# HGRN2 levels of the first four heads dealt under the f and q projections of the other four

## What is computed

```python
def hgrn2_mixer(h, w_in, lb, g_norm, w_out):
    proj = h @ w_in
    q_raw, f_raw, i_in, z = split_cols(proj, [HG_K_W, HG_K_W, HG_V_W, HG_V_W])
    q = silu(q_raw); f = lb + (1.0 - lb) * sigmoid(f_raw)
    k = 1.0 - f; logf = log(f); v = i_in          # 8 heads, 128 keys, 128 values
    ...
    # per head: o_t = sum over s <= t of (q_t * prod_{s<r<=t} f_r) . k_s  v_s
    o = o * rsqrt(mean(o * o) + EPS)
    o = o * g_norm
    return (o * silu(z)) @ w_out
```

## Time and profile before

| what | us |
|---|---|
| median of 3 runs (lowest to highest) | 358.63 (356.74 to 360.58) |
| profiled execution, its own time | 356.69 |
| span of the profiled execution | 354.2 |
| TensorE, VectorE, ScalarE, GpSimd busy | 332.1, 233.6, 181.8, 89.7 |
| level stretch | about 269 to 312 |

### The profile page before, as it was taken

One profiled execution on the slowest core, in us unless ns is written; L12 is line 12 of the kernel. 1 busy time (PEld: TensorE's weight loads), 2 busy tenths in 40 slices (PEclk: granted clock), 3 DMA queues, 4 the chain that ended last, 5 costly groups with the idle time before them and its releaser, 6 DMA issues.

```text
span 354.2 us, 5694 instructions
## 1 busy us (share of the span) xinstructions
PE 332.1 (94%) x2157; PEld 281.1 (79%) x2157; DVE 233.6 (66%) x396; ACT 181.8 (51%) x372; POOL 89.7 (25%) x83
## 2 busy tenths in 40 slices
PE   8999779999989969789899999999999999999993
PEld 5789577878979945466568878999999999889882
DVE  3884693566657779675634872744485997799942
ACT  4950556455564597775705654836473010067721
POOL 2012003343201134463420010022061575533000
PEclk9999989999999999999999999999999999999999
DMA  7999699542749000420430277671656015001011
GB/s 288 370 200 295 251 305 212 196 135 104 150 91 217 20 1 2 134 103 3 160 138 0 62 265 262 211 264 35 223 220 240 0 49 190 2 0 43 18 60 59
DMA packets 28474, 49.37 MB, mean 139 GB/s; under 512 B 3160, under 2 KB 7648, under 8 KB 28448
## 3 DMA queue, kind: packets, MB, share of 16 engines
q1 hardware_dynamic: 25696, 44.82, 40.6%
q10 hardware_dynamic: 2240, 2.17, 3.1%
q0 software_dynamic: 512, 2.03, 1.6%
HBM read 47.97 MB, written 1.05 MB: 138 GB/s over the span
## 4 chain that ended last, share of the span: by engine, by line
PE 66%; DVE 13%; ACT 8%; DMA 7%; issue 3%; POOL 1%; SPq 1%; DVEq 0%; ACTq 0%
PE bank L611 62%; DMA raw<-in_nsa 7%; DVE w_lo L1103 5%; PE bank L791 2%; ACT w_hi L882 2%; ACT prob L1002 1%; DVE nmax L1311 1%; POOL prob L532 1%; PE bank L711 1%; ACT h_hi L889 1%; DVE prob_t L1323 1%; ACT w_hi L908 1%; PE bank L852 0%; DVE zT L1232 0%; DVE zT L1233 0%
## 5 line engine op out<-in xcount | busy, mean ns | idle before, releaser
L1103 DVE TENSOR_TENSOR w_lo<-raw,w_hi 128x1024 fp32r<-128x1024 f32 (+1 forms) x80 | 93.1, 1207 | 39.8 <-ACT w_hi L882 39.8
L611 PE MATMUL bank<-w_hi,h_hi 128*128 128x512 f32 x192 | 77.0, 407 | 3.0 <-DVE w_lo L1103 2.3
L882 ACT ACTIVATE w_hi<-raw 128x1024 fp32r<-128x1024 f32 (+1 forms) x80 | 72.7, 971 | 12.4 <-DMA raw<-in_nsa 10.5
L611 PE MATMUL bank<-w_lo,h_hi 128*128 128x512 f32 x192 | 75.3, 392 | 0.0
L611 PE MATMUL bank<-w_hi,h_lo 128*128 128x512 f32 x192 | 75.2, 392 | 0.0
L611 PE MATMUL bank<-h_hi,w_hi 128*128 128x256 f32 x224 | 64.0, 286 | 0.3 <-DVE w_lo L1103 0.2
L611 PE MATMUL bank<-h_hi,w_lo 128*128 128x256 f32 x224 | 63.4, 283 | 0.0
L611 PE MATMUL bank<-h_lo,w_hi 128*128 128x256 f32 x224 | 63.4, 283 | 0.0
L611 PEld LDWEIGHTS bank<-w_hi,h_hi 128*128 128x128 f32 x192 | 36.0, 188 | 13.8 <-issue 6.2
L611 PEld LDWEIGHTS bank<-h_hi,w_hi 128*128 128x128 f32 x224 | 42.9, 192 | 0.8 <-DVE w_lo L1103 0.7
L611 PEld LDWEIGHTS bank<-h_lo,w_hi 128*128 128x128 f32 x224 | 43.0, 192 | 0.1
(11 more groups left out here) (195 smaller groups left out, 463.9 us busy)
## 6 DMA issues: line engine op xcount, KB each, us to landing
raw<-in_hg SPq DMA_DIRECT2D x16, 1024.0 KB, 7.0
raw<-in_nsa SPq DMA_DIRECT2D x12, 1024.0 KB, 12.6
raw<-in_nsa_out SPq DMA_DIRECT2D x8, 512.0 KB, 8.2
raw<-in_hg_out SPq DMA_DIRECT2D x4, 1024.0 KB, 7.0
raw<-in_nsa SPq DMA_DIRECT2D x4, 512.0 KB, 6.6
w<-in_w1k SPq DMA_DIRECT2D x2, 1024.0 KB, 11.2
w<-in_w1v ACTq DMA_DIRECT2D x2, 1024.0 KB, 16.8
x_res<-in_x SPq DMA_DIRECT2D x2, 512.0 KB, 5.2
```

What stands on the lines that cost most here:

```text
L611: return nc.tensor.matmul(o, lhsT, rhs, start=start, stop=stop, skip_group_check=True)
L882: m = nc.scalar.activation(dst, src, ACT.Copy)
L1103: m = V.tensor_tensor(lo, src, hi.bitcast(F32), ALU.subtract)
```

## The change

The schedule now does all eight levels of half 0 first, two slices of V_F1 and then of V_Q1 ahead of each level; then all eight of half 1, with one or two slices of the gate projection ahead of each (1, 2, 1, 2, ...; 12 in all). The counters of `qa_up` and `kb_up` are waited for in the new order. GpSimd's block totals of half 1 are made at the end of V_Q1 instead of V_F1. `SPREAD` deals the splits of V_F1, V_Q1, V_Z0 and V_Z1 anew.

```diff
-    for hh, (uf, uq) in enumerate(((V_F0, V_Q0), (V_F1, V_Q1))):
-        pb(uf, 0, 2)
-        pb(uf, 1, 3)
-        pb(uq, 0, 0)
-        pb(uq, 1, 1)
+    for m2 in range(2):
+        pb(V_F0, m2, 2 + m2)
+    for m2 in range(2):
+        pb(V_Q0, m2, m2)
     zs = [(("pa", u, t, sl), 2 * (u - V_Z0) + t) for u, t in Z_ORDER for sl in range(4)]
-    slot = 0
-    for lv in range(len(STEPS_L)):
-        for hh in range(2):
+    under = ([(("pb", V_F1, m2, sl), 2 + m2) for m2 in range(2) for sl in range(4)]
+             + [(("pb", V_Q1, m2, sl), m2) for m2 in range(2) for sl in range(4)],
+             zs[:12])
+    for hh in range(2):
+        done = 0
+        for lv in range(len(STEPS_L)):
+            for n in range((lv + 1) * len(under[hh]) // len(STEPS_L) - done):
+                step, bank = under[hh][done]
+                add(*step, banks=(bank,))
+                done += 1
             for c in range(TT):
                 add("lev", lv, hh, c, banks=(4 + 2 * hh + c,))
-            if slot % 4 != 3:
-                step, bank = zs.pop(0)
-                add(*step, banks=(bank,))
-            slot += 1
+    zs = zs[12:]
...
-          V_V1: (0, 0, 1, 1), V_F0: (0, 0, 0, 0), V_Q0: (0, 0, 1, 3), V_F1: (0, 4, 4, 5),
-          V_Q1: (1, 2, 2, 4), V_Z0: (0, 0, 2, 3), V_Z1: (3, 4, 11, 23), V_O0: (0, 3, 5, 8),
+          V_V1: (0, 0, 1, 1), V_F0: (0, 0, 0, 0), V_Q0: (0, 0, 1, 3), V_F1: (0, 2, 4, 5),
+          V_Q1: (1, 3, 5, 7), V_Z0: (2, 5, 8, 11), V_Z1: (2, 5, 8, 11), V_O0: (0, 3, 5, 8),
...
-                        pe.wait_ge(qa_up, 2 * (lv - 2) + hh + 1)
-                        pe.wait_ge(kb_up, 2 * (lv - 2) + hh + 1)
+                        pe.wait_ge(qa_up, 7 * hh + lv - 1)
+                        pe.wait_ge(kb_up, 7 * hh + lv - 1)
...
-                    elif kind == "pb" and step[1] in (V_F0, V_F1) and step[2] == 1:
-                        hh = int(step[1] == V_F1)
+                    elif kind == "pb" and step[1] in (V_F0, V_Q1) and step[2] == 1:
+                        hh = int(step[1] == V_Q1)
                         pool.wait_ge(f_lin, hh + 1)
```

More of the change, by code:

```diff
@@ L1386, in _ @@
                                 else:
-                                    dve.wait_ge(qa_up, 2 * (lv - 2) + hh + 1)
+                                    dve.wait_ge(qa_up, 7 * hh + lv - 1)
                                     dve.wait_ge(ft_up, 7 * hh + lv - 1)
@@ L1482, in _ @@
                         else:
-                            pool.wait_ge(kb_up, 2 * (lv - 2) + hh + 1)
+                            pool.wait_ge(kb_up, 7 * hh + lv - 1)
                             pool.wait_ge(ft_up, 7 * hh + lv - 1)
```

## The result

The changed kernel takes 362.59 us (median of 16 runs, 360.41 to 365.11), the kernel before 358.66 (16 runs). The ratio is 1.011, with a 95% interval of 1.0084 to 1.0137: about 3.9 us slower. The forecast was 362.0 and 0.9% slower; the range of 359.0 to 365.4 holds the time.

The account below looks back on a forecast made before the run. TensorE, streaming without a gap in the level stretch, was taken to bound the kernel; uncovered waits of 1.07 + 0.72 + 0.64 + 0.2 + 0.3 + 0.5 = 3.4 us, put on the median, gave 362.0 us, range 359.0 to 365.4.

Parts of the forecast that it names:

- The chain, K + 1.03: From level to level: slice start to kb 0.32, kb lasting K, qa ending 0.56 later, TensorE back after 0.15 us.
- B2: Half B (half 1, heads 4 to 7), level 1 to 2, one slice as cover: a wait of 1.07 us.
- B4: Half B, level 3 to 4, one slice as cover: a wait of 0.72 us.
- B6: Half B, level 5 to 6, one slice as cover: a wait of 0.64 us.
- Levels with two slices in half B: Ahead of half B's levels 3, 5 and 7: chain 2.43 us at most against cover 2.83, so no wait.
- A1: Half A (half 0, heads 0 to 3), level 0 to 1, a split between VectorE's two products: wait 0.2 us.
- A2: Half A, level 1 to 2, a split between the two copies: a wait of 0.3 us (0 to 0.9).
- B1: Half B, level 0 to 1: 0.33 us, up to 1.4 more if a split meets GpSimd; taken as 0.5.
- A4: Half A, level 3 to 4, VectorE also doing the other half's f work: 4.55 against 4.66 us, no wait.
- clearly slower: Rival: splits and GpSimd's queue land in the chain, waits of 5.9 us in all, 364.5 us; chance 0.29.
- The weights and the tail: Later weight transfers still land in time, no wait (bound 0 to 1 us); cross, o and output projection keep their order.
- The clock: Waits of 0.2 to 1.1 us leave TensorE's clock alone; rival with a falling clock about 372 us, chance 0.02.

Follow-up runs that it names:

- The cut products: Two runs of the changed kernel, most of half B's qa product (VectorE) or kb product (GpSimd) left out: changed stretch 71.9 and 71.2 us, against 73.7.
- e_clean_splits: Changed kernel with the splits of V_Q1, V_Z0 and V_Z1 placed behind a level's second chunk, none between chunks: 1.0053 of the kernel before.
- e_combined: Changed kernel with half B's slices dealt 0, 2, 2, 2, 2, 2, 1, 1, splits behind second chunks, half B's f and k work later: 1.0036 of before.
- e_sixteen: Changed kernel with all 16 gate slices under half B's levels, two ahead of each: 113.8 us from first V_F1 matmul to last matmul's end.
- e_old_spread: Changed kernel with the weight splits of V_F1, V_Q1, V_Z0 and V_Z1 at their old places: 1.0151 of the kernel before.
- e_f_late: Changed kernel with half B's f and k work on VectorE put behind half A's level 3 qa product: changed stretch 73.0 us, against 73.7.
- e_small_qa: Changed kernel with half B's qa product behind levels 1 to 7 cut to one block of one head: changed stretch 71.9 us, against 73.7.

## Why the prediction was right
- *What bounds the kernel.* Right: nothing was there to be saved, TensorE having been busy for 69.47 of 69.5 us, and the change uncovered waits.
- *The chain, K + 1.03.* Right in form and size. B2 1.04 for 1.07, B4 0.68 for 0.72, B6 0.59 for 0.64: the return of 0.15 was read behind a kb product, and behind qa it takes 0.10. The cut products show it to be a sequence of GpSimd and VectorE; in the prediction this was read from the end times alone.
- *Levels with two slices in half B.* Right, nothing above 0.1 at B3, B5 and B7.
- *A1, A2 and B1, the splits in VectorE's order.* 0.14, 0.26 and 0.58 for 0.2, 0.3 and 0.5; e_clean_splits took all three away. At B1 the 0.5 was a guess between 0.33 and 1.4, and its nearness to 0.58 is in part luck: the split did not start ahead of the kb, as assumed, but 0.57 behind it (288.72 against 288.15), and took 1.56 us instead of 1.18.
- *A4.* Here the step failed: "no wait, but no room either". The term was 0.56 and not 0, and without it the loss (3.9 less 0.56) would have stayed under 1%. The 2.1 us of f and k work were taken from a place where GpSimd only built block totals, which left k at its 0.69; begun 0.29 behind a kb product, it takes 0.84 more. The argument about the two engines was at hand and was not carried over to this instruction.
- *The sum.* 3.4 forecast; 3.29 without A4, 3.85 with it, 4.2 in the stretch, 3.9 between the medians. The 0.3 over the waits is of the size that the prediction named and set to zero for more switches between slices and levels, but it is not these: the slow second matmul behind a wait makes it, and in e_combined, with more switches than the kernel before (31 for 27), the stretch less its three waits of 1.5 us is 69.0, no longer than before.
- *The rival "clearly slower".* Its places (B's level 0 at 0.9 more, 0.3 each at A's levels 3 and 6 and before B's level 3, K of 2.25 at width 1) did not come up. Its idea, that what stands ahead on VectorE is paid, holds at A4, which it did not list.
- *The weights and the tail.* Right: no wait for `w_lo` of V_Z1, nothing moved behind the levels.
- *The clock.* Waits of up to 1.04 us left the granted clock of the stretch at 1.00, as forecast. In e_sixteen it fell to 0.50 when TensorE had been idle for 2.1 and then for 3.0 of 8.0 us. That is a pause far longer than any that the change makes, and says nothing for waits of 0.1 to 1 us.
- *Whether it can be told.* The prediction took a change of under 1% for about what can't be told from none. The interval of 1.0084 to 1.0137 does tell this 1.1% from none.

## What to carry to other kernels
Where one engine is busy without a gap, count for every dependent pair of steps what stands between them, and compare it with the chain's length; a reordering that keeps all work can only change these differences. Where a long GpSimd product such as kb is under way when a VectorE instruction on SBUF data is ready, count with VectorE's end after GpSimd's, and do so for every instruction of the list, not only for those of the chain. Work that is moved to cover one chain was covering another: look there before moving it.

## What the runs showed that was not expected
- Executions of one kernel differ by whether TensorE is granted half its clock for 6.8 us in the attention stretch (127.7 to 134.5): 2.6 us in the profile of the kernel before taken again, 2.5 in the changed one. In the profiles of e_old_spread and e_f_late it is there too, in e_small_qa for 3.4 us, in the others not. The spread of the times goes with the clock: of the 50 executions of the kernel before that go into the ratios of the experiments, the 18 with a mean granted clock of 0.992 or more have spans of 353.8 to 355.8 us, the 16 with 0.985 or less 356.7 to 358.8. What decides it stays open.
- `kb<-fg`, one input and one output in SBUF, took 1.53 us beside GpSimd's product and 0.69 without it. So a VectorE instruction with a single SBUF input waited too, though not beside `ft<-fg`.
- A VectorE product of one element per partition took 1.02 us beside a GpSimd product: the wait is counted as busy time of VectorE, so its busy share (66% before) holds time in which it did nothing.
